# Second mixer: the sparse branch's two heads turned together, one of them in an idle bank, two pairs behind

## The chip, the cores and the metric

One Trainium2 chip, one core. The metric is the device time of one launch in microseconds (us). The kernel before was timed three times: 1879.36, 1880.10 and 1879.52 us, median 1879.52.

## The reference

Four layers run one after another on 256 tokens of width 1024, in float32: two layers of a first kind (feed-forward, mixer, feed-forward) and two of a second kind (a mixer with three branches, then a feed-forward). The change lies in the mixer of the second kind, which is run twice. Cut to what matters, it computes

```
h = rms_norm(x); z = h @ w_in                      # q, k, v of each branch, gates, merge
# sparse branch, 8 heads in 2 groups, 4 blocks of 64 keys (all of them are selected):
o = g0 * softmax(q k_cmp) v_cmp + g1 * softmax(q k_s) v_s + g2 * softmax(q k_w) v_w
# gated linear branch (GLA), 4 heads; memory branch, 4 heads over 256 memory rows
merged = sum_b sigmoid(merge_b + b_merge_b) * (o_b @ w_branch_b)
x = x + merged @ w_out
```

With 256 tokens the selected and the windowed attention both are plain causal attention, on different keys and values. So the sparse branch is 16 causal attention heads (8 heads, for each of the two key sets) plus the small compressed attention, whose keys are 15 pooled blocks.

## The kernel before, in words

All weights stream from HBM in pieces of 128 x 1024 float32. SyncE issues a DMA into a ring of 7, ScalarE rounds a piece to its high part (`hi`, L1509), GpSimd subtracts to get the low part (`lo`, L634), and TensorE multiplies each piece in 12 matmuls of 512 columns (L661 to L663). A *strip* of the mixer's input projection is four pieces and fills two PSUM banks: banks 0 and 1 for a strip of even number, banks 2 and 3 for an odd one. The other two of these four are then the *idle banks* (`idle_banks`): the strip before stood there and has to be evicted first. Banks 4 and 5 (`SCORE`) hold scores, bank 6 (`TURNED`) transposed tiles, bank 7 (`OUT`) outputs.

`mix2_work` is a table written out by hand: behind each of the four pieces j0 to j3 of a strip it lists steps of the branches. `mix2_order` makes of it one list that all engine programs walk in the same order, each doing its own part. So the order of work on each engine's in-order queue is fixed by this table, and the engines meet only by semaphores. Strips "merge" 0 to 5 and "gr" are the last seven, then come the rows pieces of the three branches' output products, `("rows", 2, i)` first.

A head of the sparse branch passes these steps: TensorE scores for two heads at once (`nsa_score`, L958, 8 matmuls); VectorE adds the mask and finds the minimum (`minima`, L2251), writing to `soft[:, slot, 0]`; ScalarE exponentiates (L1675); VectorE normalises (`normalise`, L2258 and L2262); TensorE transposes three 128 x 128 blocks into bank TURNED (`turn_blocks`, L935); VectorE copies them to `soft[:, slot, 1]` (`take_turned`, L2270); TensorE multiplies two heads by the values (`causal_outs`, L945, 12 matmuls, with 2 matmuls L1329 of the compressed part in every other pair). Then ScalarE and VectorE make the high and low part of the output (L1680, L2241). There are 17 units (`nsa_unit`): unit 0 is the compressed attention, units 1 to 16 are heads. In the kernel before, each unit is turned in the step behind its own, one head per step, always in bank TURNED, with one set of probability buffers per slot.

Beside it run the steps of the GLA branch. `("decay", hp, i)` are long VectorE operations (L2562, L2571, L2572) with ScalarE exponentials between them. `("gla_unit", hp, m)` first does `gla_out` for m - 1 (L1223, L1225, into bank TURNED, copied out by VectorE in L2581), then 32 score matmuls (L1204), half of them in the SCORE banks and half in the idle banks, that VectorE reads in 8 masked copies (L2600). Its PSUM banks count as free when semaphore `gread` has counted these copies.

The waits of TensorE that this text speaks of: `evicted(i)`, before strip i starts, waits for the eviction of strip i - 2 (`z_merge` counts those of the merge strips, done by VectorE in L2782; `z_gr` is that of strip gr, a Silu of ScalarE in L1862, which itself waits for all `gread` of the layer); `wait_free("idle")`, before a strip starts, waits for whoever reads the idle banks; the first rows piece of branch 2 needs `z_merge` for its first 128 tokens and `z_gr` for the second; the first rows piece of branch 0 waits for semaphore `branch`, which VectorE counts up in L2722. VectorE's step `("gla", 3)` is L2532; ScalarE's is the 8 squares at L1811, behind the activation tables' load.

Of the kernel before, what the change touches and what calls it, by code (L numbers as in the profile page):

```python
# [66 lines left out]
BAND_SLOT = (3, 0, 1)  # L67
NSA_UNITS = 17

# [61 lines left out]
def mix2_work():  # L131

    windows, prep, mem, memory_in, gla, nsa = (
        [(name, i) for i in range(9)] for name in ("windows", "prep", "mem", "memory_in", "gla", "nsa"))
    cmp = [("cmp", k // 4, k % 4) for k in range(8)]
    mu = [("mem_unit", t) for t in range(6)]
    gu = [[("gla_unit", hp, m) for m in range(MT + 1)] for hp in range(2)]
    decay = [[("decay", hp, i) for i in range(4)] for hp in range(2)]
    nu = [("nsa_unit", t) for t in range(NSA_UNITS + 2)]
# [169 lines left out]
class Views:  # L309


    def __init__(self, M):
# [3 lines left out]
        def cell(n):  # L316
# [327 lines left out]
def pe_program(M, V, sem):  # L644
# [485 lines left out]
    def mix2(layer, c0, turn_next):  # L1130
# [180 lines left out]

        def nsa_turn(u):
            if u == 0:
                pe.wait_ge(sem["cprob"], layer + 1)
                wait_free("turned")
                for m in range(MT):
                    t = pe.transpose(psum[:, TURNED, m * P:m * P + P], V.pc[:, m * P:m * P + P], V.ident)
                t.then_inc(sem["cturn"], 1)
                free["turned"] = ("cpt", layer + 1)
                return  # L1320
            turn_blocks(u % 2, BLOCKS)

# [12 lines left out]
        for step in mix2_order():  # L1335
# [73 lines left out]
            elif what == "nsa_unit":  # L1409
                t = step[1]  # L1410
                if t in (0, 1, 3):
                    nsa_score(t)
                if t % 2 == 0 and t >= 4:
                    nsa_outs(t - 3)
                    if t + 1 < NSA_UNITS:
                        nsa_score(t + 1)
                if 0 <= t - 1 < NSA_UNITS:
                    nsa_turn(t - 1)
            elif what == "rows":
# [57 lines left out]
def act_program(M, V, sem, landed):  # L1477
# [188 lines left out]

    def exponentials(slot, segments):

        prob = soft[:, slot, 0, :]
        mn, total = V.stat[slot][0:2]  # L1670
# [98 lines left out]
    def mix2(layer, c0, rstd):  # L1769
# [51 lines left out]
        for step in mix2_order():  # L1821
# [77 lines left out]
            elif what == "nsa_unit":  # L1899
                t = step[1]  # L1900
                if t == 0:
                    act.wait_ge(sem["cshift"], layer + 1)
                    act.activation(V.pc, V.pc, ACT.Exp, scale=-1.0).then_inc(sem["cexp"], 1)
                elif t % 2 and t < NSA_UNITS:
                    exponentials(1, SEG)
                    exponentials(0, SEG)
                if t % 2 == 0 and t >= 4:
                    o, j = nxt("o", 2), (t - 3) // 4
                    if t % 4 == 2:
                        col = S * (j % 2)  # L1910
                        high_part(y_hi[:, Y2_TILE[0] + j, :], psum[:, OUT, col:col + S], ("o", o), "y2hi")
            elif what == "rows":
                round_piece(piece[step] + AHEAD)
# [127 lines left out]
def dve_program(M, V, sem):  # L2041
# [200 lines left out]

    def minima(slot, tables, segments, scores=None):

        prob, mn = soft[:, slot, 0, :], V.stat[slot][0]
        if not scores:
            dve.wait_ge(sem["score"], nxt("score"))
        wait_used(prob_used, slot)
        for i, ((col, width), table) in enumerate(zip(segments, tables)):
# [3 lines left out]

    def normalise(slot, segments, gates):
        prob = soft[:, slot, 0, :]
        total, inverse = V.stat[slot][1:3]
# [173 lines left out]
    def mix2(layer, c0, rstd):  # L2430
# [254 lines left out]

        def nsa_unit(t):
            if t == 0:
                cmp_probs()
            elif t % 2 and t < NSA_UNITS:
                minima(1, (V.causal[:, P:S], V.causal), SEG)  # L2690
            if t % 2 == 0 and t >= 4:
                for slot in (1, 0):
                    pt_used[slot] = ("o", nxt("o"))
                if t % 4 == 2:
                    j = (t - 3) // 4
                    col = S * (j % 2)
                    kt = Y2_TILE[0] + j
                    low_part(y_lo[:, kt, :], psum[:, OUT, col:col + S], y_hi[:, kt, :], "y2hi", "y2lo")
            if t == 1:
                dve.wait_ge(sem["cturn"], layer + 1)  # L2700
                dve.tensor_copy(V.pct, psum[:, TURNED, 0:S]).then_inc(sem["cpt"], 1)
            elif 1 <= t - 1 < NSA_UNITS:
                take_turned((t - 1) % 2, 384)
            if t % 2 and t < NSA_UNITS:
                minima(0, (V.causal[:, P:S], V.causal), SEG)
            if t == 0:
                cmp_finish()
            elif t < NSA_UNITS:
                j, b, g = (t - 1) // 4, (t - 1) // 2 % 2, (t - 1) % 2
                at = (1 + b) * 8 + 2 * j + g  # L2710
                normalise(t % 2, SEG, [V.gates[:, m, at:at + 1] for m in range(MT)])

# [23 lines left out]
        for step in mix2_order():  # L2736
# [70 lines left out]
            elif what == "nsa_unit":  # L2807
                nsa_unit(step[1])
            elif what == "branch":
# [269 lines left out]
```

## Time and profile before

| what | us |
|---|---|
| median of 3 runs | 1879.52 |
| the profiled execution | 1880.13 |
| its span | 1878.7 |
| TensorE matmul busy | 1872.5 |
| VectorE busy | 1033.4 |
| ScalarE busy | 1035.0 |
| GpSimd busy | 1555.6 |

The span is the time from the first to the last instruction; 1.4 us of the profiled execution lie around it. The busy share of TensorE says little by itself, since matmuls overlap and their ends are modelled: the distance from one start to the next is what a matmul costs. The two mixers of the second kind lie 454.4 us apart (the same step of the second layer starts that much later).

### The profile page before, as it was taken

How to read it: one execution, taken by the hardware profiler on the slowest of the kernel's cores; microseconds unless marked ns; L12 is line 12 of the kernel's file. 1: busy time of each engine (PE TensorE's matmuls, PEld its weight loads, DVE VectorE, ACT ScalarE, POOL GpSimd, SP SyncE). 2: the span in 40 equal slices, each digit the busy share in tenths (PEclk: the TensorE clock that was granted, in tenths of full speed). 3: DMA queues.
4: the chain of work that ended last, by engine and by line, in shares of the span. 5: the costliest groups of instructions: out<-in, count | busy, mean ns of one | idle time of the engine just before them, and what ended most of it. 6: DMA issues, size and time to landing. Idle time of an engine off the chain costs nothing.

```text
span 1878.7 us, 27088 instructions
## 1 busy us (share of the span) xinstructions
PE 1872.5 (100%) x9604; PEld 1549.8 (82%) x9604; DVE 1033.4 (55%) x2654; ACT 1035.0 (55%) x1765; POOL 1555.6 (83%) x1102
## 2 busy tenths in 40 slices
PE   9999999999999999999999999999999999999999
PEld 8888887888888889788888877888888877788887
DVE  5338565434676756554344677446444477645542
ACT  7445666444744576654466454665456554566543
POOL 8988886988798878698879787779887968778986
DMA  7665444565565553367556343456657533345553
GB/s 285 243 231 182 166 135 157 192 198 192 204 236 196 190 169 135 132 220 261 196 187 255 124 146 117 154 184 220 235 191 260 169 126 133 124 165 194 192 197 138
DMA packets 98419, 348.94 MB, mean 186 GB/s; under 512 B 13260, under 2 KB 13932, under 8 KB 97772
## 3 DMA queue, kind: packets, MB, share of 16 engines
q1 hardware_dynamic: 97708, 346.06, 54.0%
q8 instruction: 77, 1.26, 0.3%
q10 hardware_dynamic: 576, 1.14, 0.2%
q14 instruction: 58, 0.48, 0.1%
HBM read 346.11 MB, written 1.05 MB: 185 GB/s over the span
## 4 chain that ended last, share of the span: by engine, by line
PE 99%; DVE 1%; ACT 0%; issue 0%; ACTq 0%
PE psum L661 28%; PE psum L663 28%; PE psum L662 28%; PE psum L689 1%; PE psum L691 1%; PE psum L692 1%; PE psum L945 1%; PE psum L759 1%; PE psum L935 1%; PE psum L958 1%; PE psum L1204 1%; PE psum L925 0%; PE psum L1361 0%; PE psum L1155 0%; PE psum L832 0%; PE psum L828 0%
## 5 line engine op out<-in xcount | busy, mean ns | idle before, releaser
L634 POOL TENSOR_TENSOR lo<-raw,hi 128x256 fp32r<-128x256 f32 (+2 forms) x1070 | 1520.4, 1443 | 298.3 <-ACT hi L1509 270.4
L1509 ACT ACTIVATE hi<-raw 128x1024 fp32r<-128x1024 f32 (+1 forms) x613 | 639.1, 1052 | 495.7 <-PE psum L663 461.6
L661 PE MATMUL psum<-hi,h_hi 128*128 128x512 f32 (+1 forms) x1504 | 592.6, 394 | 0.0
L663 PE MATMUL psum<-hi,h_lo 128*128 128x512 f32 (+1 forms) x1504 | 583.6, 388 | 0.0
L662 PE MATMUL psum<-lo,h_hi 128*128 128x512 f32 (+1 forms) x1504 | 583.0, 388 | 0.0
L2211 DVE STREAM_TRANSPOSE psum<-big 32x128 f32<-32x128 f32 (+1 forms) x960 | 344.0, 358 | 14.2
L661 PEld LDWEIGHTS psum<-hi,h_hi 128*128 128x128 f32 x1504 | 282.5, 188 | 59.0 <-issue 2.1
L663 PEld LDWEIGHTS psum<-hi,h_lo 128*128 128x128 f32 x1504 | 282.3, 188 | 58.9
L661 PE MATMUL psum<-hi,y_hi 128*128 128x512 f32 x832 | 328.1, 394 | 0.0
L662 PEld LDWEIGHTS psum<-lo,h_hi 128*128 128x128 f32 x1504 | 282.7, 188 | 54.8
L663 PE MATMUL psum<-hi,y_lo 128*128 128x512 f32 x832 | 324.3, 390 | 0.0
L662 PE MATMUL psum<-lo,y_hi 128*128 128x512 f32 x832 | 323.9, 389 | 0.0
L2220 DVE TENSOR_TENSOR y_lo<-psum,y_hi 128x512 fp32r<-128x512 f32 x76 | 51.0, 689 | 327.8 <-ACT y_hi L1635 327.4
L661 PEld LDWEIGHTS psum<-hi,y_hi 128*128 128x128 f32 x832 | 156.2, 188 | 34.5 <-issue 2.5
L663 PEld LDWEIGHTS psum<-hi,y_lo 128*128 128x128 f32 x832 | 156.2, 188 | 33.1
L662 PEld LDWEIGHTS psum<-lo,y_hi 128*128 128x128 f32 x832 | 156.3, 188 | 31.1
L2199 DVE SCALAR_TENSOR_TENSOR big<-psum,small,big 128x256 f32<-128x256 f32 (+1 forms) x120 | 61.0, 550 | 87.9 <-ACT big L1625 87.8
L1675 ACT ACTIVATE soft<-soft,small 128x128 f32<-128x128 f32 (+1 forms) x104 | 47.2, 455 | 78.3 <-DVE small L2251 57.5
L1625 ACT ACTIVATE big<-psum,small 128x256 f32<-128x256 f32 (+1 forms) x120 | 57.3, 529 | 53.9 <-PE psum L663 53.8
L2270 DVE COPY soft<-psum 128x384 f32<-128x384 f32 (+1 forms) x52 | 29.8, 573 | 49.3 <-PE psum L935 49.3
L689 PE MATMUL psum<-h_hi,hi 128*128 128x256 f32 x192 | 56.1, 292 | 0.0
L691 PE MATMUL psum<-h_lo,hi 128*128 128x256 f32 x192 | 54.3, 283 | 0.0
(355 smaller groups left out, 1599.4 us busy)
## 6 DMA issues: line engine op xcount, KB each, us to landing
raw<-in_stream SPq DMA_DIRECT2D x607, 512.0 KB, 3.4
big<-in_w SPq DMA_DIRECT2D x14, 512.0 KB, 7.1
big<-in_post SPq DMA_DIRECT2D x6, 512.0 KB, 4.7
special<-in_b_merge SPq DMA_DIRECT2D x2, 1536.0 KB, 7.4
raw<-in_stream SPq DMA_DIRECT2D x8, 296.0 KB, 5.6
memkv<-in_mem_turned SPq DMA_DIRECT2D x2, 1024.0 KB, 6.9
big<-in_band SPq DMA_DIRECT2D x2, 768.0 KB, 4.9
raw<-in_first SPq DMA_DIRECT2D x2, 512.0 KB, 4.1
```

What stands on the lines that cost most here:

```text
L634: t = pool.tensor_tensor(M.lo[:, slot, w], M.raw[:, slot, w], f32(M.hi[:, slot_hi, w]), ALU.subtract)
L661: pe.matmul(out, lhs_hi, rhs_hi, start=start, stop=False)
L662: pe.matmul(out, lhs_hi, rhs_lo, start=False, stop=False)
L663: return pe.matmul(out, lhs_lo, rhs_hi, start=False, stop=stop)
L689: pe.matmul(out, hi[:, slot_hi, w], h_hi[:, k, :], start=k == 0 and block % 2 == 0, stop=False, skip_group_check=True)
L691: pe.matmul(out, hi[:, slot_hi, w], h_lo[:, k, :], start=False, stop=False, skip_group_check=True)
L1509: act.activation(M.hi[:, slot_hi, used], M.raw[:, slot, used], ACT.Copy).then_inc(sem["hi"], 1)
L1625: t = act.activation(act_s[:, m, :], psum[:, bank + m, 0:width], ACT.Silu if gated else ACT.Relu, scale=V.scale[:, m:m + 1])
L1675: t = act.activation(prob[:, w], prob[:, w], ACT.Exp, scale=-1.0, bias=mn[:, i:i + 1], accum_out=total[:, i:i + 1])
L2199: t = dve.scalar_tensor_tensor(prod_s[:, m, :], psum[:, bank + m, col:col + width], V.scale[:, m:m + 1], act_s[:, m, :], ALU.mult, ALU.mult)
L2211: t = dve.transpose(dst[32 * b:32 * b + 32, :, :, 32 * a:32 * a + 32], src[32 * a:32 * a + 32, :, :, 32 * b:32 * b + 32])
L2220: dve.tensor_tensor(flat(y_lo[:, kt:kt + 2, :]), psum[:, bank + g, :], f32(flat(y_hi[:, kt:kt + 2, :])), ALU.subtract).then_inc(sem["ylo"], 1)
```

## The change

The 17 units become one compressed unit and 8 pairs. Step `nsa_pair k` does, on TensorE, the outputs of pair k - 3, the scores of pair k and the transposes of both heads of pair k - 2; the head of slot 1 goes to bank TURNED, that of slot 0 to the first idle bank (for the last two pairs, to bank SCORE[0]). Before it writes the idle bank, TensorE waits for the eviction of the strip before. The probabilities of even and odd pairs lie in two buffer sets (`soft` and the first 768 columns of `big`). Normalising is a step of its own, one or two pieces behind the pair. On VectorE a pair step does both minima, then both copies of turned blocks; a pair's minima wait for the transposes of the pair that last used the buffers. The table is written anew: there are pair steps at j0 of most strips instead of unit steps at every second piece.

```diff
-        ("merge", 0): ([gla[2], nu[0]], [decay[0][0]], [nu[1], decay[0][1]], none),
-        ("merge", 1): ([nu[2], decay[0][2]], [nu[3]], [decay[0][3]], [nu[4]]),
-        ("merge", 2): (none, [nu[5]], [gu[0][0]], [nu[6]]),
-        ("merge", 3): (none, [nu[7]], [gu[0][1]], [nu[8], decay[1][0]]),
-        ("merge", 4): ([gu[0][2], nu[9], decay[1][1]], [nu[10]], [nu[11], decay[1][2]], [nu[12], decay[1][3]]),
-        ("merge", 5): (none, [nu[13]], [gu[1][0]], [nu[14]]),
-        "gr": (none, [nu[15]], [gu[1][1]], [nu[16]]),
-        ("rows", 2): ([nu[17]], [nu[18], gu[1][2]], [gla[3]], [gla[4], gla[5]]),
+        ("merge", 0): ([gla[2], cmp_unit], [decay[0][0]], [pair[0], decay[0][1]], [norm[0]]),
+        ("merge", 1): ([decay[0][2]], [pair[1]], [norm[1], decay[0][3]], none),
+        ("merge", 2): ([pair[2]], [norm[2]], [gu[0][0]], none),
+        ("merge", 3): ([pair[3]], [norm[3]], [gu[0][1]], [decay[1][0]]),
+        ("merge", 4): ([gu[0][2], pair[4], decay[1][1]], [norm[4]], [pair[5], decay[1][2]], [norm[5], decay[1][3]]),
+        ("merge", 5): ([pair[6]], [norm[6]], [gu[1][0]], none),
+        "gr": ([pair[7]], [norm[7], pair[8]], [gu[1][1]], none),
+        ("rows", 2): (none, [gu[1][2], pair[9]], [pair[10], gla[3]], [gla[4], gla[5]]),
...
+        self.nsa_prob = [[M.soft[:, slot, 0, 0:384] for slot in range(2)],
+                         [big[:, 384 * slot:384 * slot + 384] for slot in range(2)]]
...
+        def second_bank(k):
+            last = k + PAIRS_AHEAD >= NSA_PAIRS
+            return (0, SCORE[0]) if last else ("idle", idle_banks(strip_now)[0])
+
+        def turn_pair(k):
+
+            for slot in (1, 0):
+                prob = V.nsa_prob[k % PAIRS_AHEAD][slot]
+                pe.wait_ge(sem["prob"], nxt("prob"))
+                name, bank = ("turned", TURNED) if slot else second_bank(k)
+                if name == "idle":
+                    evicted(strip_now + 1)
+                wait_free(name)
+                for i, col in enumerate(BLOCKS):
+                    t = pe.transpose(psum[:, bank, i * P:i * P + P], prob[:, col:col + P], V.ident)
+                t.then_inc(sem["pturn"], 1)
+                free[name] = ("pt", nxt("taken"))
+
+        def nsa_pair(k):
+            if k > PAIRS_AHEAD:
+                nsa_outs(2 * (k - PAIRS_AHEAD) - 1)
+            if k < NSA_PAIRS:
+                nsa_score(2 * k + 1)
+            if k == 0:
+                cmp_turn()
+            if 0 <= k - PAIRS_AHEAD < NSA_PAIRS:
+                turn_pair(k - PAIRS_AHEAD)
...
+        def nsa_pair(k, strip):
+            done, turned = k - PAIRS_AHEAD - 1, k - PAIRS_AHEAD
+            if done >= 0:
+                for slot in (1, 0):
+                    pt_used[slot] = ("o", nxt("o"))
+            if k < NSA_PAIRS:
+                for slot in (1, 0):
+                    used = n["pturn"] + 2 - slot if turned >= 0 else None
+                    minima(slot, (V.causal[:, P:S], V.causal), SEG, prob=V.nsa_prob[k % PAIRS_AHEAD][slot], used=used)
...
+            if 0 <= turned < NSA_PAIRS:
+                take_turned(1, 384)
...
+                bank = idle_banks(strip)[0] if k < NSA_PAIRS else SCORE[0]
+                dve.tensor_copy(soft[:, 0, 1, 0:384], psum[:, bank, 0:384]).then_inc(sem["pt"], 1)
+            if done >= 0 and done % 2:
...
+                low_part(y_lo[:, kt, :], psum[:, OUT, col:col + S], y_hi[:, kt, :], "y2hi", "y2lo")
+
+        def nsa_norm(k):
+            for slot in (1, 0):
+                at = (1 + k % 2) * 8 + 2 * (k // 2) + 1 - slot
+                normalise(slot, SEG, [V.gates[:, m, at:at + 1] for m in range(MT)], V.nsa_prob[k % PAIRS_AHEAD][slot])
```

## Rows read from the trace of the kernel before

**Rows 1.** The page: busy time by engine, and the chain that ended last.
```profile
PE 1872.5 (100%) x9604; PEld 1549.8 (82%) x9604; DVE 1033.4 (55%) x2654; ACT 1035.0 (55%) x1765; POOL 1555.6 (83%) x1102
...
PE 99%; DVE 1%; ACT 0%; issue 0%; ACTq 0%
```

**Rows 2.** All waits of TensorE: who for whom, us in total, times, longest.
```profile
PE psum L935 <- DVE big L2581: 1.2, 2, 0.6
```

**Rows 3.** Timeline, TensorE, merge 1 behind j0: start us, us, engine, line, operation, count.
```profile
1090.50 0.39 PE L663 MATMUL psum<-hi,h_lo 128*128 128x512 f32 x1
1090.73 0.49 PE L935 MATMUL psum<-consts,soft 128*128 128x128 f32 x3
1090.97 0.48 PE L661 MATMUL psum<-hi,h_hi 128*128 128x512 f32 x1
1091.29 0.40 PE L662 MATMUL psum<-lo,h_hi 128*128 128x512 f32 x1
```

**Rows 4.** Timeline, TensorE, merge 2 behind j3: outputs, scores and one turn.
```profile
1116.47 0.39 PE L663 MATMUL psum<-hi,h_lo 128*128 128x512 f32 x1
1116.79 0.88 PE L945 MATMUL psum<-soft,big 128*64 128x128 f32 x12
1117.59 0.93 PE L958 MATMUL psum<-kT,qT 64*128 64x128 f32 x8
1118.45 0.55 PE L935 MATMUL psum<-consts,soft 128*128 128x128 f32 x3
1118.75 0.48 PE L661 MATMUL psum<-hi,h_hi 128*128 128x512 f32 x1
```

**Rows 5.** Timeline, TensorE, merge 4 behind j0: end of gla_out, then a turn.
```profile
1139.27 0.39 PE L1225 MATMUL psum<-big,extra 128*128 128x128 f32 x2
1140.27 0.52 PE L935 MATMUL psum<-consts,soft 128*128 128x128 f32 x3 [0.61 <-DVE big L2581]
```

**Rows 6.** Busy time in two stretches: PE, PEld, DVE, ACT, POOL, clock, DMA.
```profile
1087.30:1104.40 17.10, 17.10 (x97) 13.30 (x96) 16.99 (x42) 13.55 (x26) 12.93 (x13) 1.00 0.48 154
1147.90:1163.50 15.60, 15.60 (x98) 12.34 (x98) 15.20 (x35) 9.72 (x22) 13.07 (x16) 1.00 0.41 135
```

**Rows 7.** Timeline, VectorE, strips merge 1 and 2: copy, eviction of merge 1, normalising.
```profile
1092.17 0.55 DVE L2270 COPY soft<-psum 128x384 f32<-128x384 f32 x1
...
1103.07 1.40 DVE L2782 SCALAR_TENSOR_TENSOR big<-psum,small,special 128x512 f32<-128x512 f32 x2
...
1105.04 1.13 DVE L2262 TENSOR_SCALAR soft<-soft,small,extra 128x128 f32<-128x128 f32 x2
```

**Rows 8.** Timeline, merge 5: the GLA scores behind j2, and VectorE's masked copies.
```profile
1162.28 0.39 PE L663 MATMUL psum<-hi,h_lo 128*128 128x512 f32 x1
...
1164.58 0.50 PE L661 MATMUL psum<-hi,h_hi 128*128 128x512 f32 x1
...
1163.80 3.10 DVE L2600 COPY_PREDICATED big<-special,psum 128x128 f32<-128x128 int32 x8 [0.32 <-PE psum L1204]
```

**Rows 9.** Timeline, strip gr's end and the first rows pieces: PE, DVE, ACT.
```profile
1183.75 0.39 PE L663 MATMUL psum<-hi,h_lo 128*128 128x512 f32 x1
...
1185.61 0.48 PE L661 MATMUL psum<-hi,y_hi 128*128 128x512 f32 x1
...
1180.68 3.08 DVE L2600 COPY_PREDICATED big<-special,psum 128x128 f32<-128x128 int32 x8
...
1194.60 1.23 DVE L2532 TENSOR_TENSOR big<-big 128x1024 f32<-128x1024 f32 x1
...
1197.81 2.59 DVE L2722 TENSOR_TENSOR big<-big,psum 128x512 f32<-128x512 f32 x4 [1.99 <-PE psum L663]
...
1183.84 1.28 ACT L1862 ACT_TABLE_LOAD   x1 [4.39 <-DVE big L2600]
1185.14 1.27 ACT L1862 ACTIVATE big<-psum,small 128x512 f32<-128x512 f32 x2
...
1197.93 0.31 ACT L1811 ACTIVATE big<-big 128x128 f32<-128x128 f32 x1
```

More of the change, by code:

```diff
@@ L67 @@
 BAND_SLOT = (3, 0, 1)
-NSA_UNITS = 17
+NSA_PAIRS = 8
+PAIRS_AHEAD = 2
 Y1_EVENT = {3: 1, 4: 1, 5: 2, 6: 3, 7: 4, 0: 5, 1: 6, 2: 7}
@@ L138, in mix2_work @@
     decay = [[("decay", hp, i) for i in range(4)] for hp in range(2)]
-    nu = [("nsa_unit", t) for t in range(NSA_UNITS + 2)]
+    cmp_unit = ("nsa_unit", 0)
+    pair = [("nsa_pair", k) for k in range(NSA_PAIRS + PAIRS_AHEAD + 1)]
+    norm = [("nsa_norm", k) for k in range(NSA_PAIRS)]
     none = ()
@@ L1310, in nsa_score, with cmp_turn @@
             causal_scores(1, qT[:, j, :], kT[:, b, :])
[L1312 to L1321, printed above, removed]
+        def cmp_turn():
+            pe.wait_ge(sem["cprob"], layer + 1)
+            wait_free("turned")
+            for m in range(MT):
+                t = pe.transpose(psum[:, TURNED, m * P:m * P + P], V.pc[:, m * P:m * P + P], V.ident)
+            t.then_inc(sem["cturn"], 1)
+            free["turned"] = ("cpt", layer + 1)
+        def second_bank(k):
[22 more added lines that the diff above has]
+                turn_pair(k - PAIRS_AHEAD)
         def nsa_outs(u):
@@ L1409, in mix2 @@
             elif what == "nsa_unit":
[L1410 to L1418, printed above, removed]
+                nsa_score(0)
+            elif what == "nsa_pair":
+                nsa_pair(step[1])
             elif what == "rows":
@@ L1665, in turn_qk, with exponentials @@
                            scale=scale).then_inc(sem["qk"], 1)
-    def exponentials(slot, segments):
-        prob = soft[:, slot, 0, :]
+    def exponentials(slot, segments, prob=None):
+        prob = soft[:, slot, 0, :] if prob is None else prob
         mn, total = V.stat[slot][0:2]
@@ L1899, in mix2 @@
             elif what == "nsa_unit":
[L1900 to L1909, printed above, removed]
+                act.wait_ge(sem["cshift"], layer + 1)
+                act.activation(V.pc, V.pc, ACT.Exp, scale=-1.0).then_inc(sem["cexp"], 1)
+            elif what == "nsa_pair":
+                k = step[1]
+                done = k - PAIRS_AHEAD - 1
+                if done >= 0:
+                    o, j = nxt("o", 2), done // 2
+                    if done % 2:
                         col = S * (j % 2)
                         high_part(y_hi[:, Y2_TILE[0] + j, :], psum[:, OUT, col:col + S], ("o", o), "y2hi")
+                if k < NSA_PAIRS:
+                    for slot in (1, 0):
+                        exponentials(slot, SEG, V.nsa_prob[k % PAIRS_AHEAD][slot])
             elif what == "rows":
@@ L2241, in low_part, with minima @@
         dve.tensor_tensor(out, src, f32(high), ALU.subtract).then_inc(sem[name_lo], 1)
-    def minima(slot, tables, segments, scores=None):
-        prob, mn = soft[:, slot, 0, :], V.stat[slot][0]
+    def minima(slot, tables, segments, scores=None, prob=None, used=None):
+        prob, mn = soft[:, slot, 0, :] if prob is None else prob, V.stat[slot][0]
         if not scores:
             dve.wait_ge(sem["score"], nxt("score"))
-        wait_used(prob_used, slot)
+        if used:
+            dve.wait_ge(sem["pturn"], used)
+        else:
+            wait_used(prob_used, slot)
         for i, ((col, width), table) in enumerate(zip(segments, tables)):
@@ L2252, in minima, with normalise @@
                                      ALU.add, ALU.min, mn[:, i:i + 1]).then_inc(sem["mn"], 1)
-    def normalise(slot, segments, gates):
-        prob = soft[:, slot, 0, :]
+    def normalise(slot, segments, gates, prob=None):
+        prob = soft[:, slot, 0, :] if prob is None else prob
         total, inverse = V.stat[slot][1:3]
@@ L2684, in cmp_finish @@
                               ALU.mult).then_inc(sem["cprob"], 1)
[L2686 to L2691, printed above, removed]
+        def nsa_pair(k, strip):
+            done, turned = k - PAIRS_AHEAD - 1, k - PAIRS_AHEAD
+            if done >= 0:
                 for slot in (1, 0):
                     pt_used[slot] = ("o", nxt("o"))
[L2694 to L2699, printed above, removed]
+            if k < NSA_PAIRS:
+                for slot in (1, 0):
+                    used = n["pturn"] + 2 - slot if turned >= 0 else None
+                    minima(slot, (V.causal[:, P:S], V.causal), SEG, prob=V.nsa_prob[k % PAIRS_AHEAD][slot], used=used)
+            if k == 0:
@@ L2700, in nsa_unit @@
                 dve.wait_ge(sem["cturn"], layer + 1)
                 dve.tensor_copy(V.pct, psum[:, TURNED, 0:S]).then_inc(sem["cpt"], 1)
[L2702 to L2711, printed above, removed]
+            if 0 <= turned < NSA_PAIRS:
+                take_turned(1, 384)
+                dve.wait_ge(sem["pturn"], nxt("pturn"))
+                prob_used[0] = ("pturn", n["pturn"])
+                wait_used(pt_used, 0)
+                bank = idle_banks(strip)[0] if k < NSA_PAIRS else SCORE[0]
+                dve.tensor_copy(soft[:, 0, 1, 0:384], psum[:, bank, 0:384]).then_inc(sem["pt"], 1)
@@ L2713, in branch @@
+            if done >= 0 and done % 2:
+                j = done // 2
+                col, kt = S * (j % 2), Y2_TILE[0] + j
+                low_part(y_lo[:, kt, :], psum[:, OUT, col:col + S], y_hi[:, kt, :], "y2hi", "y2lo")
[3 more added lines that the diff above has]
+                normalise(slot, SEG, [V.gates[:, m, at:at + 1] for m in range(MT)], V.nsa_prob[k % PAIRS_AHEAD][slot])
         def branch(b, m):
@@ L2807, in mix2 @@
             elif what == "nsa_unit":
-                nsa_unit(step[1])
+                cmp_probs()
+                cmp_finish()
+            elif what == "nsa_pair":
+                nsa_pair(step[1], strip_now)
+            elif what == "nsa_norm":
+                nsa_norm(step[1])
             elif what == "branch":
```

## The prediction

> **What bounds the kernel now.** First the page: the chain that ended last is 99% TensorE, which is busy for 1872.5 of 1878.7 us [rows 1]. So the time is the sum of TensorE's issue distances plus its stalls, and an edit counts only as far as it changes one of these. Second the waits of TensorE: in both second mixers there is one that the change touches, a turn (L935) waiting for VectorE's L2581, twice 0.6 us [rows 2]. Third the timeline of TensorE between two stream matmuls, for what a detour costs. Last VectorE and ScalarE in the same stretches, for when they would answer if TensorE came earlier. Times below are those of layer 0's mixer in the kernel before; the second layer repeats them, so each sum is doubled.
>
> **Unit prices on TensorE.** Stream matmuls start 0.23 us apart, so a piece of 12 costs 2.73. A lone turn of three blocks: from the last stream matmul before it to the second after it 0.79 us instead of 0.455, so 0.34 [rows 3]. Inside a longer detour outputs take 0.80, scores 0.86, a turn 0.30 [rows 4]; entering costs 0.09 more than a stream start (0.32 against 0.23), leaving another 0.09 (0.32 against 0.23, as in [rows 3]). A second turn right behind the first I take at 3 x 0.107 = 0.32, an estimate between 0.30 and 0.34. The two L1329 cost 0.44: strip gr's detour takes 1.86 us in all [rows 9], less 0.32, 0.80 and 0.30.
>
> **What goes.** (1) Seven turns per layer stood alone in the table (units 1, 4, 6, 10, 12, 14, 16); each joins another turn: 7 x (0.34 - 0.32), with bounds of 0 and 0.3: -0.2. The number of other detours is ten before and ten after, so no entering or leaving is saved. (2) Unit 8's turn stood right behind gla_out in the same bank. It starts 1.00 us after the last L1225 group, where 0.22 would do (two matmuls of 0.11) [rows 5]: -0.78 per layer. In the new order outputs and scores (1.66 us) stand between, longer than the copy it waits for. Together -0.98 per layer. This is all that can be gained: the matmuls, transposes and VectorE operations are otherwise the same in number.
>
> **What comes: idle bank at merge 2.** Pair 2 at j0 turns its second head into the banks of merge 1, so it waits for that eviction. TensorE: until 1090.50 nothing changes [rows 3]; then j1 (2.73), pair 1's scores (0.86 + 0.18), three pieces (8.19) and 0.32 + 0.86 + 0.32 for entering, scores and first turn: it is there at 1103.96. VectorE is busy for 16.99 of 17.10 us before the end of this eviction [rows 6], which starts at 1103.07 and ends at 1104.47 [rows 7]. Its new order has ahead of it two copies less (turns 1 and 2, 0.47 each with overlap) and one normalisation more (0.15 + 1.13, some 1.24): +0.3, so 1104.8. Stall 0.85 (0 to 1.8).
>
> **GLA scores at merge 5.** They fill the idle banks behind j2, and strip gr may start there only when VectorE has read them (0.23 + 2.19 + 2.73 = 5.1 us later, no detour now stands between; before, unit 14's did, some 2.2 us). The reading ended at 1166.90, while the detour began at 1162.28 and a start without unit 14's detour would be at 1167.4 [rows 8]: a margin of 0.5, if VectorE is ready at 1163.8. In the new order it has, from pair 5's turn to this read, four minima, four copies, four normalisations, two decay halves, an eviction and a low part. The nearest stretch of before has four minima, three copies, three normalisations, the same two decay halves and eviction in 15.6 us, 0.3 of it idle [rows 6]; with 0.47 + 1.3 + 0.35 more that is 17.4, and with latency 0.15 and the read (3.1) 20.6. If its four normalisations took 1.24 each as in [rows 7], and not the 1.5 that this stretch leaves for one, it is 19.7, by estimate. TensorE goes from the end of that first turn to strip gr's start in 0.32 + 5.46 + 2.48 (pair 6) + 5.46 + 2.19 + 2.73 + 0.1 = 18.7 us. Stall 1.0 to 1.9; I take 1.4, bounds 0 and 2.8: 0.35 us more or less for each normalisation, an estimate from the same difference.
>
> **Strip gr's eviction.** Between gr's last piece and the first rows piece stood a detour of 1.86 [rows 9], now nothing. The second token half of that piece waits for z_gr. ScalarE's table load starts at 1183.84, 0.08 after VectorE's last read of gu[1][1] (1180.68 + 3.08), and its two Silu end at 1186.41 [rows 9]. These follow TensorE's own GLA scores and stay. TensorE now starts the rows at 1183.98 and reaches the second half six matmuls later, at 1185.35, against 1186.45. Stall 1.1 (0.8 to 1.3). The trace shows 1.28 us for the load and the Silu right behind it [rows 9]. The Trainium skill (ScalarE: Activation LUTs, What ACT_TABLE_LOAD costs) gives about 2.66 us with the drain for a switch of sets. By that the eviction would end 1.4 us later and the stall be 2.5; the trace disagrees.
>
> **Rows of branch 0.** The last outputs move one piece back, to j2 of the rows pieces. ScalarE reaches their high part when its squares started before, at 1197.9 less 0.3 for the earlier high part that has gone [rows 9]; VectorE's low part ends at 1198.4, L2532 (1.23, before at 1194.60, in idle time) at 1199.6, so the first `branch` comes at 1200.3 instead of 1197.81 + 0.69 = 1198.5 [rows 9]. TensorE: second half at 1186.52, rows piece 0's last matmul 1187.66, j1 2.73, detour of gla_out (some 0.8, by estimate eight matmuls of 0.11 less overlap), outputs, L1329, two turns and the change-overs 2.95, j2 2.73, last outputs 1.0, j3 2.73, next start 1200.03. Stall 0.35 (0 to 0.8).
>
> **Sum.** Per layer -0.98 + 0.85 + 1.4 + 1.1 + 0.35 = +2.7, twice +5.4 us: the profiled execution goes from 1880.13 to 1885.5, and the median, which lies 0.6 lower, from 1879.52 to 1884.9.
>
> At nothing I cost the weight stream (ScalarE may be held in a pair's exponentials by some 3 us of late minima, but it rounds four pieces, 10.9 us, ahead) and the buffer waits `pturn`, which TensorE fulfils in the same detour. Pair 8's outputs need pair 5's copies, done some 1.9 us after its turns, with 2.8 to spare. If one of these covers is gone, it costs its excess alone.
>
> **Rivals.** (a) VectorE keeps up: both stalls on it vanish, the two at the end stay. -0.98 + 1.1 + 0.35 = +0.5 per layer, median 1880.5. For it: normalising takes 1.13 us in [rows 7] and VectorE's stretches with a busy GpSimd (12.93 and 13.07 us in [rows 6]) are the slow ones, so other phases could be faster. Against: GpSimd's stream is the same. The Trainium skill (SBUF — State Buffer, SBUF: two separate sides) has VectorE and GpSimd exclude each other for a whole instruction at a shared port. By that these durations depend on who starts first, and (a) or (c) could come from phase alone.
> (b) Not slower, everything is covered: GLA reads, Silu and `branch` come as early as TensorE does, only the removed stall counts. 2 x -0.98, median 1877.6. It decides at z_gr: it needs ScalarE's load ahead of VectorE's last read, and the load follows that read by 0.08 us. A gain over 0.2% has no source in the sum.
> (c) VectorE falls further behind and all waits reach their upper bounds: -0.98 + 1.8 + 2.8 + 1.3 + 0.8 = 5.7 per layer, median 1890.9. For it: VectorE had next to no idle time in either stretch [rows 6], so every added operation is paid in full.
> (d) The detours shrink by more than I price, because grouped transposes pipeline better: at 0.24 per turn seven would save 0.7 per layer, median 1883.9. That lies within my forecast's own range.
>
> **How the numbers follow.** Forecast with (d) 0.57 (own range 1882.5 to 1887.5), (a) 0.20, (b) 0.08, (c) 0.15. The range 1880.4 to 1889.5 leaves out (b) and about half of (a)'s and (c)'s outer parts. Changes under 0.2% (3.8 us) can't be told from none. Slower by more: nine tenths of the forecast and (c), 0.66. Same: the rest of the forecast, (a) and most of (b), 0.31. Faster: 0.03.
>
> **What would show it.** No wait of L935 on L2581; a wait on L2782 before L935 in merge 2, of about 0.85; one on L2600 at gr's start of about 1.4; one on L1862 in the middle of the first rows piece of about 1.1; one on L2722 at the first rows piece of branch 0. Seven detours fewer. The prediction is wrong if the first two are not there, or if TensorE waits at a place not named.

## The result, and the profile after

The changed kernel takes 1887.83 us (median of 5 runs, 1887.28 to 1888.73), the kernel before 1879.49 in runs taken beside it (5 runs, 1879.28 to 1880.10). The ratio is 1.0044, with a 95% interval of 1.0031 to 1.0057: 8.3 us slower. The forecast was 1884.9 with a range from 1880.4 to 1889.5. One slow execution of the kernel before (6843.82 us at a granted clock of 0.382, beside e1 to e4 below) is left out of all comparisons. Line numbers have shifted by the change: stream matmuls are L666 to L668, scores L963, outputs L950, turns L1339, the merge strips' eviction L2812, normalising L2286 and L2290, decay halves L2590, L2599 and L2600, masked reads of the GLA scores L2628, the Silu L1886, `branch` L2752, GpSimd's low parts L639, ScalarE's rounding L1533.

The page after, busy time by engine and the chain that ended last; they answer to [rows 1].

```profile
PE 1875.1 (99%) x9604; PEld 1548.5 (82%) x9604; DVE 1037.0 (55%) x2654; ACT 1034.1 (55%) x1765; POOL 1553.9 (82%) x1102
...
PE 95%; DVE 4%; issue 1%; ACT 1%; DVEq 0%; ACTq 0%
```

The same 9604 matmuls; what is new is 5% of the chain on other engines. The waits of TensorE after (who for whom, us in total, times, longest), against [rows 2]:

```profile
PE psum L666 <- issue: 2.2, 2, 1.1
PE psum L666 <- ACT big L1886: 1.9, 2, 0.9
PE psum L1339 <- DVE big L2812: 1.5, 2, 0.8
```

The old wait of a turn for gla_out's copy is no longer in the list, and three new ones are there, each once per layer. Because both kernels issue the same 7008 stream matmuls in the same order, they can be laid side by side by number: the distance between the two starts grows by 3.9 us over the second-kind mixer of layer 0 and by 4.2 over that of layer 1, and by -0.3 in all the rest (0.42 more between the mixers, and 0.76 less before the first stream matmul). So the mixers hold the loss: 8.1 us of it. The old wait of 0.6 is gone in layer 0; in layer 1 a rest of 0.13 us stays at the same turn.

The places, all of layer 0, in order of time. First merge 2 behind j0, TensorE and then VectorE; it answers to [rows 3, 7].

```profile
1102.73 0.93 PE L963 MATMUL psum<-kT,qT 64*128 64x128 f32 x8
1103.58 0.55 PE L1339 MATMUL psum<-consts,soft 128*128 128x128 f32 x3
1104.91 0.52 PE L1339 MATMUL psum<-consts,soft 128*128 128x128 f32 x3 [0.78 <-DVE big L2812]
...
1103.37 1.40 DVE L2812 SCALAR_TENSOR_TENSOR big<-psum,small,special 128x512 f32<-128x512 f32 x2
```

The second turn could start at 1103.90; it starts 1.01 later, 0.14 after the eviction ends. Only 0.78 of this is shown as idle, since the end of a matmul is modelled: the distance of starts is the price. From the stream matmul ahead of this detour to the first behind it are 2.77 us, and 1.81 in the runs below where no wait is left: the wait costs 0.96.

Then merge 5 and the start of strip gr, TensorE and VectorE; it answers to [rows 8].

```profile
1165.26 0.39 PE L668 MATMUL psum<-hi,h_lo 128*128 128x512 f32 x1
1166.76 0.47 PE L666 MATMUL psum<-hi,h_hi 128*128 128x512 f32 x1 [1.11 <-issue]
...
1161.44 0.67 DVE L2290 TENSOR_SCALAR soft<-soft,small,extra 128x128 f32<-128x128 f32 x2
1162.03 0.16 DVE L2286 RECIPROCAL small<-small 128x2 f32<-128x2 f32 x1
1162.22 1.45 DVE L2290 TENSOR_SCALAR soft<-soft,small,extra 128x128 f32<-128x128 f32 x2
1163.60 3.07 DVE L2628 COPY_PREDICATED big<-special,psum 128x128 f32<-128x128 int32 x8
```

The distance of the two starts is 1.50 where 0.23 is normal. The page calls the releaser "issue", but TensorE goes on 0.09 us after VectorE's last masked read has ended at 1166.67, and these reads stand right behind pair 6's two normalisations with no idle time between.

Third the middle of the first rows piece, TensorE and ScalarE, a distance of 1.32; it answers to [rows 9].

```profile
1186.62 0.39 PE L668 MATMUL psum<-hi,y_lo 128*128 128x512 f32 x1
1187.94 0.50 PE L666 MATMUL psum<-hi,y_hi 128*128 128x512 f32 x1 [0.93 <-ACT big L1886]
...
1185.33 1.28 ACT L1886 ACT_TABLE_LOAD   x1 [4.38 <-DVE big L2628]
1186.62 1.26 ACT L1886 ACTIVATE big<-psum,small 128x512 f32<-128x512 f32 x2
```

Fourth the first rows piece of branch 0, TensorE and VectorE, also against [rows 9]: a distance of 0.47, where the first L2752 ends at about 1201.8.

```profile
1201.44 0.39 PE L668 MATMUL psum<-hi,y_lo 128*128 128x512 f32 x1
1201.91 0.50 PE L666 MATMUL psum<-hi,y_hi 128*128 128x512 f32 x1
...
1199.57 0.42 DVE L2266 TENSOR_TENSOR y_lo<-psum,y_hi 128x256 fp32r<-128x256 f32 x1 [3.56 <-ACT y_hi L1704]
1199.91 1.22 DVE L2560 TENSOR_TENSOR big<-big 128x1024 f32<-128x1024 f32 x1
1201.16 2.48 DVE L2752 TENSOR_TENSOR big<-big,psum 128x512 f32<-128x512 f32 x4
```

And a fifth that was not forecast, in merge 1: the first matmuls of two pieces come 0.44 and 0.51 us after the matmul ahead of them. GpSimd meanwhile has no gap for 24 us, after 3.88 us of idling for ScalarE. VectorE's first operation of decay half 3, ahead of the eviction, takes 1.76 us. The last two rows are GpSimd's and VectorE's of the kernel before, at the same places.

```profile
1096.26 0.39 PE L668 MATMUL psum<-hi,h_lo 128*128 128x512 f32 x1
1096.70 0.50 PE L666 MATMUL psum<-hi,h_hi 128*128 128x512 f32 x1
...
1099.32 0.39 PE L668 MATMUL psum<-hi,h_lo 128*128 128x512 f32 x1
1099.83 0.47 PE L666 MATMUL psum<-hi,h_hi 128*128 128x512 f32 x1
...
1091.78 24.27 POOL L639 TENSOR_TENSOR lo<-raw,hi 128x256 fp32r<-128x256 f32 x27 [3.88 <-ACT hi L1533]
1100.01 1.76 DVE L2599 TENSOR_TENSOR memkv<-big 128x1024 f32<-128x1024 f32 x1
...
1092.55 23.95 POOL L634 TENSOR_TENSOR lo<-raw,hi 128x256 fp32r<-128x256 f32 x27 [3.88 <-ACT hi L1509]
1100.26 1.21 DVE L2571 TENSOR_TENSOR memkv<-big 128x1024 f32<-128x1024 f32 x1
```

### The profile page after: what moved, and what is told of

Its sections match the earlier page's. It is cut to its first block, busy times and chain, and to the rows that moved or that the text cites. A ratio compares the mean times of both kernels' runs of the same rounds, so it can differ in the third digit from the quotient of the medians.

```text
span 1886.4 us, 27090 instructions
## 1 busy us (share of the span) xinstructions
PE 1875.1 (99%) x9604; PEld 1548.5 (82%) x9604; DVE 1037.0 (55%) x2654; ACT 1034.1 (55%) x1765; POOL 1553.9 (82%) x1102
## 3 DMA queue, kind: packets, MB, share of 16 engines
q8 instruction: 77, 1.26, 0.3%
## 4 chain that ended last, share of the span: by engine, by line
PE 95%; DVE 4%; issue 1%; ACT 1%; DVEq 0%; ACTq 0%
PE psum L666 27%; PE psum L668 27%; PE psum L667 27%; PE psum L694 1%; PE psum L696 1%; PE psum L697 1%; PE psum L950 1%; PE psum L764 1%; PE psum L1209 1%; PE psum L963 1%; PE psum L1339 1%; DVE big L2590 0%; PE psum L930 0%; PE psum L1391 0%; PE psum L940 0%
## 5 line engine op out<-in xcount | busy, mean ns | idle before, releaser
L639 POOL TENSOR_TENSOR lo<-raw,hi 128x256 fp32r<-128x256 f32 (+2 forms) x1070 | 1518.7, 1442 | 308.4 <-ACT hi L1533 280.6
L1533 ACT ACTIVATE hi<-raw 128x1024 fp32r<-128x1024 f32 (+1 forms) x613 | 638.4, 1052 | 495.4 <-PE psum L668 464.2
L666 PE MATMUL psum<-hi,h_hi 128*128 128x512 f32 (+1 forms) x1504 | 592.6, 394 | 2.7 <-issue 2.2
L668 PE MATMUL psum<-hi,h_lo 128*128 128x512 f32 (+1 forms) x1504 | 583.7, 388 | 0.0
L666 PEld LDWEIGHTS psum<-hi,h_hi 128*128 128x128 f32 x1504 | 282.5, 188 | 65.5 <-issue 7.7
L668 PEld LDWEIGHTS psum<-hi,h_lo 128*128 128x128 f32 x1504 | 282.3, 188 | 59.0
L666 PE MATMUL psum<-hi,y_hi 128*128 128x512 f32 x832 | 328.5, 395 | 2.0 <-ACT big L1886 1.9
L668 PE MATMUL psum<-hi,y_lo 128*128 128x512 f32 x832 | 324.3, 390 | 0.0
L666 PEld LDWEIGHTS psum<-hi,y_hi 128*128 128x128 f32 x832 | 156.2, 188 | 38.6 <-issue 2.8
L668 PEld LDWEIGHTS psum<-hi,y_lo 128*128 128x128 f32 x832 | 156.1, 188 | 33.1
L1699 ACT ACTIVATE soft<-soft,small 128x128 f32<-128x128 f32 (+1 forms) x72 | 32.9, 458 | 64.6 <-DVE small L2279 44.0
L697 PE MATMUL psum<-h_hi,lo 128*128 128x256 f32 x192 | 54.3, 283 | 0.0
```

The source lines that it names most:

```text
L639: t = pool.tensor_tensor(M.lo[:, slot, w], M.raw[:, slot, w], f32(M.hi[:, slot_hi, w]), ALU.subtract)
L666: pe.matmul(out, lhs_hi, rhs_hi, start=start, stop=False)
L668: return pe.matmul(out, lhs_lo, rhs_hi, start=False, stop=stop)
L697: t = pe.matmul(out, lo[:, slot, w], h_hi[:, k, :], start=False, stop=k == KD - 1, skip_group_check=True)
L1533: act.activation(M.hi[:, slot_hi, used], M.raw[:, slot, used], ACT.Copy).then_inc(sem["hi"], 1)
```

## The experiments

All are the changed kernel with entries of its table moved, save the one that replaces the Silu. Each was run with the kernel before on the same chip; chips differ by some tenths of a us, so "against before" below is the difference of the two medians (the kernel before took 1879.91 beside e1 to e4, 1879.87 beside e5 to e8, 1879.88 beside e9 to e11). The changed kernel itself stands at +8.34. Each run's median is of 4 to 11 executions, so a difference of 0.3 us says nothing; the places are read from the traces, by the distances of starts.

| run | median | against before |
|---|---|---|
| e1_norm6 | 1885.67 | +5.76 |
| e2_gla11 | 1886.07 | +6.16 |
| e3_decay3 | 1888.53 | +8.62 |
| e4_rows | 1887.06 | +7.15 |
| e5_all (1 to 4 together) | 1882.70 | +2.83 |
| e6_copy | 1886.52 | +6.65 |
| e7_merge0 | 1888.08 | +8.21 |
| e10_decay3_m0 (3 and 7) | 1884.85 | +4.97 |
| e8_all_m0 (1 to 4 and 7) | 1879.43 | -0.44 |
| e9_pair8 | 1878.59 | -1.29 |
| e11_decay10 | 1880.62 | +0.74 |

**e1_norm6: VectorE ready for the GLA reads.**

```diff
-        ("merge", 5): ([pair[6]], [norm[6]], [gu[1][0]], none),
+        ("merge", 5): ([pair[6]], none, [gu[1][0]], [norm[6]]),
```

> The changed kernel, but normalising of pair 6 moves from merge 5 j1 to j3, behind VectorE's masked reads of the GLA scores. Theory (VectorE reaches these reads late because the normalisations, copies and decay halves lie ahead of them, and strip gr may not start before they end): in the changed kernel strip gr starts 1.27 us late plus 0.1 for the pause itself; with 2.3 us of normalising taken from in front, the reads start when the scores come, and this wait falls to 0 to 0.1: 2 x -1.35 = -2.7 us. Rival 1 (the reads are held by TensorE's own scores or by their 3.1 us, whatever stands ahead): the wait stays at 1.2, no change. Rival 2 (the normalising is only displaced and comes back as a wait of pair 6's turn at gr j1): +0.5 to +2 per layer there.

It gained 2.6 us. Side by side with the changed kernel the matmuls come 1.27 us earlier at strip gr's start and 0.08 more behind it (1.29 and 0.08 in layer 1), and no wait comes back at pair 6's turns. VectorE's reads now wait for the scores:

```profile
1162.17 3.11 DVE L2628 COPY_PREDICATED big<-special,psum 128x128 f32<-128x128 int32 x8 [0.51 <-PE psum L1209]
```

So the cause was what stood ahead of the reads, and both rivals fall.

**e2_gla11: the last GLA reads one piece earlier.**

```diff
-        "gr": ([pair[7]], [norm[7], pair[8]], [gu[1][1]], none),
+        "gr": ([pair[7]], [gu[1][1]], [norm[7], pair[8]], none),
```

> The changed kernel, but gu[1][1] (GLA scores and outputs) goes from gr j2 to j1, and normalising of pair 7 with pair 8 from j1 to j2. Theory (the Silu that evicts strip gr waits for VectorE's last GLA read, then 1.28 us of table load and 1.27 of Silu; TensorE now meets it in the middle of the first rows piece, 1.09 late): the last read comes some 4.4 us earlier, the Silu then waits for the strip's end alone and ends about 1.3 + 1.3 after it at worst; the wait falls to between 0 and 0.3 and with it the branch wait of 0.24 may fall too: 2 x (-0.8 to -1.6) = -1.6 to -3.2 us. Rival (the table load and Silu start only at the strip's end in any case and set the time): the load would start 0.5 later than now, z_gr come as late, no change or +0.5 us per layer.

It gained 2.2 us; the place itself gains 0.93 in either layer and keeps 0.16. ScalarE's rows show the new order: the table is loaded before the strip ends, and the Silu waits for TensorE alone.

```profile
1184.33 1.28 ACT L1886 ACT_TABLE_LOAD   x1
1186.49 1.27 ACT L1886 ACTIVATE big<-psum,small 128x512 f32<-128x512 f32 x2 [0.87 <-PE psum L668]
```

The branch wait did not shrink (0.26), as ScalarE's and VectorE's later chain starts from the strip's end again.

**e6_copy: the table load taken away.** In L1886 `ACT.Silu` became `ACT.Copy`. This kernel leaves out the Silu, so it does not compute the layer; it only serves to time the wait.

> The changed kernel with strip gr's Silu replaced by a copy with the same scale, so the Silu is left out of the computation and with it the load of its table (1.28 us). Theory (z_gr comes late by the chain last GLA read, table load, Silu): z_gr comes 1.28 earlier, the 1.09 wait in the first rows piece goes: 2 x -1.1 = -2.2 us. Rival (z_gr waits for the strip's end and the activation queue, and the load is hidden before it): no change.

The place gained 0.96 and 0.94 us in the two layers, as good as the same as in e2_gla11; the whole run 1.7, less than the 2.2 expected. Some 0.14 stays here too: the two passes start when the strip ends (1186.06) and take 1.26 us, to 1187.32, a little longer than TensorE needs to reach the second half of the rows piece.

```profile
1186.06 1.26 ACT L1886 ACTIVATE big<-psum,small 128x512 f32<-128x512 f32 x2 [4.77 <-PE psum L668]
```

Two different cures of the same chain give the same, so the chain (last read, load, Silu) was the cause.

**e3_decay3: the eviction of merge 1 ahead of the decay half.**

```diff
-        ("merge", 1): ([decay[0][2]], [pair[1]], [norm[1], decay[0][3]], none),
+        ("merge", 1): ([decay[0][2]], [pair[1]], [norm[1]], [decay[0][3]]),
```

> The changed kernel, but decay half 3 of the first head pair goes from merge 1 j2 to j3, so that on VectorE it stands behind the eviction of merge 1. Theory (the second head's turn in the idle bank waits 0.78 us for this eviction because VectorE does 3.4 us of decay ahead of it): the eviction comes some 1.7 us earlier or more, the wait goes: 2 x -0.9 = -1.8 us. The two starts of pieces in merge 1 that wait for the low part of the weights (0.21 and 0.28 us) would stay if they come from GpSimd, which is slowed by VectorE's long operations, or shrink if these move away: -0.3 per layer more. Rival (the decay half comes back as a wait of the GLA scores at merge 2 j2, which need it): +0.5 or more there.

A miss: nothing gained (+0.3). The turn no longer waits, the two turns run as one group, and right behind them TensorE waits for the next piece's low part.

```profile
1104.33 0.88 PE L1339 MATMUL psum<-consts,soft 128*128 128x128 f32 x6
1105.74 0.50 PE L666 MATMUL psum<-hi,h_hi 128*128 128x512 f32 x1 [0.54 <-POOL lo L639]
```

Behind VectorE's limit stood a second of the same height, GpSimd's: the eviction ended 3.4 us earlier than in the changed kernel (counted from the same stream matmul in merge 1), and TensorE lost 1.0 us here and in the next piece to the low parts instead of the 0.96. The wait on GpSimd had been hidden by that on VectorE. The rival, the GLA scores waiting for the decay half, did not appear.

**e7_merge0: ScalarE no longer held, so GpSimd gets its piece early.**

```diff
-        ("merge", 0): ([gla[2], cmp_unit], [decay[0][0]], [pair[0], decay[0][1]], [norm[0]]),
+        ("merge", 0): ([gla[2], cmp_unit], none, [pair[0], decay[0][0]], [decay[0][1], norm[0]]),
```

> The changed kernel, but decay half 0 of the first head pair stands behind pair 0's minima (merge 0 j2) and half 1 at j3. Theory (ScalarE sits 4.6 us in pair 0's exponentials behind VectorE's decay half 0, so it rounds the next weight pieces late, GpSimd idles 3.9 us for them and then runs without idle time for 23.6 us behind TensorE): one piece is rounded some 3 us earlier and GpSimd has that much lead, so the waits of 0.21 and 0.28 us at pieces of merge 1 go, with 0.1 to 0.2 of pauses: -0.6 per layer; the wait of 0.78 for the eviction of merge 1 stays within 0.5 or grows, as the decays move back: total between -1.5 and +0.5 us. Rival (GpSimd is slow, not late): it is behind again by merge 1 j2, the waits stay.

Alone it gained nothing that can be told (-0.1), within the expectation, but for the reason given there: the two late piece starts are gone (0.21 and 0.28 us less at the starts, and 0.1 less behind each), and the turn in merge 2 waits longer, 1.4 instead of 0.8. By starts the detour grows from 2.77 to 3.43, which is the 0.7 won in merge 1. The eviction itself ends when it did (counted from the same stream matmul in merge 1, within 0.1 us), although the decay halves were moved.

```profile
PE psum L1339 <- DVE big L2812: 2.9, 2, 1.4
```

GpSimd's rows in merge 0 to 2, which had one gap of 3.88 us and then none, now have gaps of about 1 us and less all along:

```profile
1082.50 9.76 POOL L639 TENSOR_TENSOR lo<-raw,hi 128x256 fp32r<-128x256 f32 x12 [5.18 <-ACT hi L1533]
1093.23 2.87 POOL L639 TENSOR_TENSOR lo<-raw,hi 128x256 fp32r<-128x256 f32 x4 [0.97 <-ACT hi L1533]
1096.43 4.63 POOL L639 TENSOR_TENSOR lo<-raw,hi 128x256 fp32r<-128x256 f32 x4 [0.33 <-ACT hi L1533]
1102.20 14.07 POOL L639 TENSOR_TENSOR lo<-raw,hi 128x256 fp32r<-128x256 f32 x16 [1.14 <-ACT hi L1533]
```

So here GpSimd was late, not too slow. It is slower in places: a piece's four parts take 2.87 us or 4.63, the latter beside VectorE's decay operations among others. The Trainium skill (SBUF — State Buffer, SBUF: two separate sides) says that a GpSimd operation and a VectorE one with two SBUF inputs exclude each other; these durations agree with that, though no run took VectorE's operations away.

**e10_decay3_m0: both at once.**

> The changed kernel with decay half 3 behind the eviction of merge 1 and the new order in merge 0, nothing else. Each alone gained nothing (+0.7 and +0.25 us). Theory (two limits of equal height in merges 1 and 2, the eviction on VectorE and the low parts on GpSimd, so that only taking away both pays): -3.2 to -3.5 us, 1884.5. Rival (what the two gained in the run with all moves came from their company): -1 or less, 1887.

-3.4 us against the changed kernel, where the two alone gave +0.3 and -0.1. The late piece starts are gone and the detour in merge 2 takes 1.81 instead of 2.77, in both layers. That shows two equal limits: each removal pays only after the other.

**e4_rows: the last pairs one rows piece earlier.**

```diff
-        ("rows", 2): (none, [gu[1][2], pair[9]], [pair[10], gla[3]], [gla[4], gla[5]]),
+        ("rows", 2): ([pair[9]], [pair[10], gu[1][2]], [gla[3]], [gla[4], gla[5]]),
```

> The changed kernel, but the last two pairs' steps come one rows piece earlier: pair 9 behind j0 and pair 10 with the GLA outputs behind j1, as the last outputs were in the kernel before. Theory (the low part of the last sparse output, held at j2 until ScalarE has loaded its table, delays VectorE's gla step 3 and through it semaphore branch, 0.24 us and 0.1 for the pause): this wait goes, one detour less is entered and left (0.2): 2 x -0.5 = -1.0 us; the z_gr wait of 1.09 stays, since it lies ahead of both. Rival (branch is late because TensorE itself is early there): the wait stays or grows by the 1 us that pair 10's outputs no longer cover, 0 to +1.5 us.

-1.2 us by the medians; in the traces the two mixers together gain 0.7, which is the branch wait alone (0.23 instead of 0.47 at that piece, 0.11 less behind it, in layer 0). The detour less that the expectation priced at 0.2 does not show as one: the table still has 15 detours, since pair 9 at j0 opens a new one where the last outputs at j2 close. The Silu wait stays, at 0.87 of shown idle time. The rival falls.

**e5_all and e8_all_m0: the moves together.**

> The changed kernel with all four moves of the runs before at once (normalising of pair 6 behind the GLA reads, gu[1][1] one piece earlier, decay half 3 behind the eviction of merge 1, pairs 9 and 10 one rows piece earlier). Theory (each wait is caused at its own place, so their removals add, and merge 1 and 2 are bound by GpSimd's low parts whichever wait shows): -1.4 -0.9 -0.5 per layer against the changed kernel, nothing for decay half 3: 2 x -2.8 = -5.6, 1882.2 us. Rival (the waits cover for each other, so TensorE arriving earlier at the next place gives the gain back there): 1884 or more.

> All four moves and the one of merge 0 together. Theory (with GpSimd's lead restored, the removal of the eviction wait by decay half 3, which gained nothing alone, is worth its 0.9 us): 2 x (-2.8 - 0.6 - 0.9) = -8.6 against the changed kernel, 1879.2 us, as fast as the kernel before. Rival (GpSimd's rate in merge 1 and 2 binds in any case): as with the four moves alone, 1882.

e5_all measured 1882.7 and e8_all_m0 1879.43 (ratio to before 0.9997, 0.9988 to 1.0006). The gains add: in the two mixers e1_norm6, e2_gla11, e4_rows and e10_decay3_m0 gained 8.42 us in all by their traces, e8_all_m0 8.65. In e8_all_m0 no wait of this change is left on TensorE but the 0.15 for the Silu and some 0.05 at one piece start in merge 3. The loss is thereby accounted for by waits at five places. The idle bank, the second buffer set and the grouping cost nothing beyond them that shows: they are all still in e8_all_m0.

**e9_pair8: a cover for the last one.**

```diff
-        "gr": ([pair[7]], [gu[1][1]], [norm[7], pair[8]], none),
+        "gr": ([pair[7]], [gu[1][1]], [norm[7]], [pair[8]]),
```

> The five moves together, and pair 8 goes on to gr j3. Theory (of the waits only the one for strip gr's Silu is left, 0.15 us and 0.1 for the pause, since nothing stands between the strip's end and the first rows piece; pair 8's detour of 1.6 us covers it): 2 x -0.25 against the five moves alone, 1878.9 us, 0.5 under the kernel before or the same within the error. Rival (pair 9, now one piece after pair 8, waits for the copies of its turned blocks): +0.5 to +1 per layer.

1878.59 us (11 runs, 1878.22 to 1878.88), beside 1879.88 (24 runs, 1879.49 to 1880.23) for the kernel before: ratio 0.9993, 0.9984 to 1.0002. No run of one reaches those of the other, but the interval still holds 1. It is the fastest version found, 9.6 us under the changed kernel. Each of its two mixers is 0.63 us shorter than before. TensorE waits for nothing in these mixers that it did not wait for before, bar one piece start:

```profile
PE psum L807 <- DVE big L2924: 1.1, 1, 1.1
PE psum L1281 <- DVE extra L2651: 1.0, 2, 0.5
PE psum L666 <- POOL lo L639: 0.2, 1, 0.2
```

**e11_decay10: a failed refinement.** On top of e9_pair8:

```diff
-        ("merge", 3): ([pair[3]], [norm[3]], [gu[0][1]], [decay[1][0]]),
-        ("merge", 4): ([gu[0][2], pair[4], decay[1][1]], [norm[4]], [pair[5], decay[1][2]], [norm[5], decay[1][3]]),
+        ("merge", 3): ([pair[3]], [norm[3]], [gu[0][1]], none),
+        ("merge", 4): ([gu[0][2], pair[4], decay[1][0]], [decay[1][1], norm[4]], [pair[5], decay[1][2]], [norm[5], decay[1][3]]),
```

> As the run with pair 8 at gr j3, and decay half 0 of the second head pair goes from merge 3 j3 to merge 4 j0 behind pair 4, half 1 to j1. Theory (VectorE copies gla_out's result late, because the decay half lies ahead of it, and pair 4's first turn waits 0.1 to 0.3 for that copy): 2 x -0.2, 1878.5 us. Rival (the decay halves now push pair 5's and pair 6's VectorE work back until the GLA scores of merge 5 wait): +0.5 or more per layer.

2.0 us slower than e9_pair8: the rival's mechanism, VectorE pushed back, but at a place ahead of the one that it named. Strip merge 5 starts 0.93 late in both layers, when VectorE has just copied pair 3's turned blocks out of the idle bank (L2732, 1148.93 + 0.54); in e9_pair8 this copy ended 1.5 us earlier, at 1148.01:

```profile
1148.42 0.39 PE L668 MATMUL psum<-hi,h_lo 128*128 128x512 f32 x1
1149.58 0.47 PE L666 MATMUL psum<-hi,h_hi 128*128 128x512 f32 x1 [0.77 <-issue]
...
1148.93 0.54 DVE L2732 COPY soft<-psum 128x384 f32<-128x384 f32 x1
```

And the detour in merge 4 takes 3.50 us from the stream matmul ahead to the one behind, as in e9_pair8: in that run there was no wait to remove. What the theory took for one lies between gla_out and the outputs, whose starts are 0.32 apart instead of 0.22: another change-over. A true wait there, of 0.1 to 0.2 us in layer 1 and at most 0.07 in layer 0, is in the changed kernel and in e1 to e7, and it is gone in e8_all_m0 and e10_decay3_m0 already.

## Why the prediction was right, and where it was short

Layer 0, by the steps of the prediction (measured: by distances of starts, for waits with the pause of 0.1 that follows them; the first row is what is left of the mixer's 3.9 when the others are taken off):

| step | forecast | measured |
|---|---|---|
| lone turns and unit 8's wait | -0.98 | -0.65 |
| idle bank at merge 2 | +0.85 | +0.96 |
| weight stream in merge 1 | 0 | +0.68 |
| GLA scores, strip gr's start | +1.4 | +1.35 |
| strip gr's eviction | +1.1 | +1.20 |
| rows of branch 0 | +0.35 | +0.35 |
| sum | +2.7 | +3.9 |

The direction and the four named waits were right, and experiments confirm their causes by removing them: e1_norm6 the GLA scores, e2_gla11 and e6_copy the eviction of strip gr, e4_rows the branch, e10_decay3_m0 the idle bank. Rival (a), VectorE keeping up, and (b), everything covered, are out: VectorE came late at both places (its busy time even rose from 1033.4 to 1037.0 us for the same 2654 operations), and z_gr came by the chain described. Rival (c) is out as far as the waits go; none reached its upper bound. Rival (d) did not appear: a second turn right behind the first costs 0.33 (a detour of 3.05 against 2.72 with one turn, 2.61 against 2.28), where 0.32 was priced and 0.24 would have been needed.

For the GLA scores both arrivals came as worked out. From the end of pair 5's first turn (1146.71) TensorE would have been at strip gr's start after 18.8 us (forecast 18.7), and VectorE's reading ended after 20.0 (forecast 19.7 to 20.6).

By its own sign the prediction was wrong in one point: TensorE waits at a place that it did not name, GpSimd's low parts in merge 1. Three things were missing, 1.2 us per layer together.

The first is "At nothing I cost the weight stream": the cover of four pieces was counted from TensorE's side as if GpSimd were always ahead. It was not: it had idled 3.88 us for ScalarE in merge 0 and then took 24.27 us for 27 parts, 3.6 per piece, against 2.73 for TensorE between detours. The kernel before had the same gap and nearly the same rate (23.95 us for 27 parts), and TensorE's three detours there gave it time (the lone turn; scores with a turn; outputs, scores and a turn); the change took most of that TensorE work out of these strips and put it later. The forecast had the row for it (GpSimd busy for 12.93 of 17.10 us) and read it only as a load on VectorE.

The idle bank's 0.85 was right by luck, in the same strips. Counted from the same stream matmul in merge 1, the eviction was forecast to end at 1104.8 and ended at 1105.54, for VectorE came 1.07 us later than before and not 0.3. The two copies less and the normalisation more took what was forecast; but one decay operation took 1.76 us instead of 1.21, and VectorE idled some 0.2 for ScalarE. TensorE was forecast to be there at 1103.96 and came at 1104.69, held by GpSimd, so that the difference came out the same. In e7_merge0 and e10_decay3_m0, without GpSimd's waits, TensorE comes at 1103.97. The two terms belong together: 1.64 us where 0.85 was forecast, and either limit alone costs as much (1.70 in e3_decay3, 1.63 in e7_merge0).

Second, each wait ahead of a stream matmul costs 0.1 more than itself: after a pause the second matmul starts 0.31 to 0.34 behind the first instead of 0.23, as after any change-over. I had priced that for detours and not for waits. In the branch row it is hidden, since the wait itself was 0.24 and not 0.35. Third, -0.98 was too much by 0.33. Of this, 0.1 is the change-over between gla_out and the outputs, and 0.13 the turns: at 0.33 for a grouped one against 0.34 for a lone one, seven save 0.07, and even the forecast's own 7 x 0.02 is 0.14, which its -0.98 took as 0.2. The remaining 0.1 was not traced to a place.

The old wait was removed but for 0.13 us in layer 1, and was worth its 0.78 per layer by the trace; no run tested it by itself. That there is a gain under the waits shows in e9_pair8, whose mixers are 0.63 us shorter than before each.

## What to carry to other kernels

When the bounding engine has no idle time, moving its side work changes who is covered: for each place from which work is taken, ask which wait it was long enough to hide, and for every engine that feeds the stream, how far it is ahead at that moment. Two waits of equal height hide each other, so one that is cured without gain may still be needed; try the pair before dropping either. Here the reordering stopped costing time, and became at best a small gain (0.07%, within the error), only when the producers' long operations were put behind, and not ahead of, the evictions and reads for which the next strip waits.

## What the runs showed of the hardware

A wait of TensorE in its stream costs its length and about 0.1 us more: the first matmul after it is followed at 0.31 to 0.34 us instead of 0.23, at all such waits of these runs. And the profile's "issue" can stand for a semaphore: the 1.11 us of "issue" at strip gr's start went when VectorE's reads came earlier. What the activation table load cost hung on where it stood: 1.28 us of load in front of the Silu cost some 0.95 in the changed kernel, by e6_copy, and nothing in e2_gla11, where it ran ahead of the strip's end. And VectorE's durations moved with the order of work: the same decay operation in merge 1 took 1.21 us before and 1.76 after.
